# Sample tokens' expert dots, the second group's query blocks and state products, and the closings of three tiles moved to other slots of a hand-written order

## What is computed

```python
q = (xb @ w_q).reshape(blk, PEER_HEADS, 2, half)            # "wq" jobs, 8 heads of 256 columns
...                                                         # q normalised per half
s = jnp.einsum('thpd,hpnd->thpn', q, keys_f)                # "scores"
s1, i1 = lax.top_k(s[:, :, 0], PEER_TOPK); s2, i2 = ...     # 16 of 128, twice
sc, ci = lax.top_k(cand, PEER_TOPK)                         # 16 of 256: the head's experts
h = jax.nn.gelu(jnp.einsum('thkd,td->thk', u_tab[idx], xb)) # "dots"
y = jnp.einsum('thk,thkd->td', gate * h, v_tab[idx])        # "sums"
x2 = LN(alpha*x1 + y);  x3 = x2 + (p @ w_pe) * sigmoid(x2 @ w_pg)   # "closing" of a tile
```

## Time and profile before

| | |
|---|---|
| median of 3 runs | 1877.51 us (1875.82 to 1878.71) |
| the profiled execution's own time | 1876.79 us |
| its span | 1875.0 us |
| busy: PE, DVE, POOL, ACT | 76%, 63%, 54%, 22% |
| DMA | 673.28 MB, mean 359 GB/s |
| mean granted TensorE clock | 0.842 of full speed |

### The profile page before, as it was taken

One profiled execution on the slowest core, in us unless ns is written; L12 is line 12 of the kernel. 1 busy time (PEld: TensorE's weight loads), 2 busy tenths in 40 slices (PEclk: granted clock), 3 DMA queues, 4 the chain that ended last, 5 costly groups with the idle time before them and its releaser, 6 DMA issues.

```text
span 1875.0 us, 20726 instructions
## 1 busy us (share of the span) xinstructions
PE 1424.7 (76%) x7144; PEld 890.3 (47%) x7144; DVE 1172.9 (63%) x3013; ACT 418.0 (22%) x848; POOL 1003.4 (54%) x1067
## 2 busy tenths in 40 slices
PE   8999999799878798989894997356643435775477
PEld 7888887676654455656461554023311001241034
DVE  1110224878877674776678665788888967776632
ACT  2320201124431122232111222111321211031022
POOL 0000000646655565665466766576777776767764
PEclk9999999899997799999896998658765666587589
DMA  7335551999999999999999999999999999999996
GB/s 293 135 122 217 223 179 52 329 413 404 411 412 412 407 413 409 407 411 411 394 395 410 379 410 413 408 408 407 407 410 409 408 407 395 395 362 410 409 396 269
DMA packets 173494, 673.28 MB, mean 359 GB/s; under 512 B 20768, under 2 KB 24480, under 8 KB 159567
## 3 DMA queue, kind: packets, MB, share of 16 engines
q0 software_dynamic: 151520, 546.94, 73.9%
q1 hardware_dynamic: 21798, 124.96, 17.1%
q10 hardware_dynamic: 72, 0.07, 0.0%
HBM read 664.48 MB, written 7.41 MB: 358 GB/s over the span
## 4 chain that ended last, share of the span: by engine, by line
PE 42%; DMA 26%; DVE 14%; POOL 10%; issue 7%; ACT 1%; SPq 0%; DVEq 0%; POOLq 0%; PEldq 0%
DMA at<-in_v_tab,idxV 18%; PE PJ L1633 14%; PE PJ L1513 7%; PE Y L1683 7%; DMA at<-in_u_tab,idx 7%; POOL at L746 5%; DVE at L1382 5%; POOL at L755 5%; PE PJ L1497 4%; PE PJ L1520 3%; PE PJ L1532 1%; DVE at L1310 1%; PE Y L1722 1%; PE PJ L1539 1%; PE PJ L1586 0%
## 5 line engine op out<-in xcount | busy, mean ns | idle before, releaser
L746 POOL DMA_INDIRECT at<-in_u_tab,idx x512 | 489.8, 957 | 556.6 <-DVEq L1365 322.7
L1382 DVE CUSTOM_DVE_ANT_0 at<-at,XD 128x1024 f32<-128x1024 f32 x512 | 615.9, 1215 | 202.7 <-DMA at<-in_u_tab,idx 189.4
L755 POOL DMA_INDIRECT at<-in_v_tab,idxV x512 | 487.6, 952 | 290.3 <-PE Y L1683 156.0
L1683 PE MATMUL Y<-at,at 128*32 128x512 f32 x1920 | 340.5, 837 | 371.3 <-DMA at<-in_v_tab,idxV 371.1
L1633 PE MATMUL PJ<-at,at 128*128 128x256 f32 (+1 forms) x1792 | 413.9, 390 | 6.3 <-DVE at L1232 2.3
L1633 PEld LDWEIGHTS PJ<-at,at 128*128 128x128 f32 x1792 | 342.0, 193 | 86.3 <-issue 23.7
L1683 PEld LDWEIGHTS Y<-at,at 128*32 128x32 f32 x1920 | 69.9, 135 | 554.8 <-issue 553.7
L1513 PE MATMUL PJ<-at,at 128*128 128x256 f32 (+2 forms) x960 | 218.5, 386 | 2.5 <-DVE at L1289 1.0
L1513 PEld LDWEIGHTS PJ<-at,at 128*128 128x128 f32 (+2 forms) x960 | 166.5, 176 | 57.7 <-issue 14.8
L1497 PE MATMUL PJ<-at,at 128*128 128x256 f32 (+1 forms) x640 | 142.0, 380 | 0.0
L1497 PEld LDWEIGHTS PJ<-at,at 128*128 128x128 f32 (+1 forms) x640 | 107.6, 170 | 36.0 <-issue 9.2
(11 more groups left out here) (237 smaller groups left out, 1350.7 us busy)
## 6 DMA issues: line engine op xcount, KB each, us to landing
at<-in_w_blk SPq DMA_DIRECT2D x72, 1024.0 KB, 7.9
at<-in_w_q SPq DMA_DIRECT2D x16, 1024.0 KB, 8.0
at<-in_w_o SPq DMA_DIRECT2D x8, 1024.0 KB, 7.3
at<-in_u_tab,idx POOLq DMA_INDIRECT x512, 11.6
at<-in_v_tab,idxV POOLq DMA_INDIRECT x512, 11.0
at<-in_state SPq DMA_DIRECT2D x4, 1024.0 KB, 8.6
out_st_s<-at SPq DMA_DIRECT2D x4, 1024.0 KB, 8.8
at<-in_w_pg SPq DMA_DIRECT2D x2, 2048.0 KB, 14.0
```

The lines of the kernel that those rows point to most:

```text
L746: pool.indirect_dma_start(ubuf[slot], None, u_tab, bass.IndirectOffsetOnAxis(rows_of, 0)).then_inc(u_in[slot], 16)
L755: pool.indirect_dma_start(vbuf[slot], None, v_tab, bass.IndirectOffsetOnAxis(rows_of, 0)).then_inc(v_in[slot], 16)
L1382: v.tensor_tensor_reduce(out=t, in0=t, in1=XD[:, :], scale=1.0, scalar=0.0, op0=ALU.mult, op1=ALU.add, accum_out=hraw[:, n % 2, k:k + 1]). ...
L1683: last = mm(Y[32 * c:32 * c + 32, s, :], wpadV[d // PAIR % 2][:, g, :], vbuf[slot][:, 512 * s:512 * s + 512], start=False, stop=final)
```

## The change

- `SAMPLE_DOTS_AT` 26, every second slot, becomes 25, every fourth slot (`SAMPLE_STEP`): samples 0 to 7 at slots (25, 0), (25, 4), ... (26, 12), two steps ("two heads") instead of one. `sample_at` says which sample stands at a slot; the gathers of GpSimd, their numbering (`u_number`, `u_sample`) and the row jobs follow it.
- `REST_AT`: the closing of tile 0 starts at slot (20, 1) instead of (18, 1), tile 1 at (22, 1) instead of (20, 1), tile 2 at (27, 6) instead of (27, 1). Tile 4 stays at (30, 1).
- `queries(1)` runs by pairs of heads, tile by tile, instead of head by head, and the 23 jobs are spread to slot (18, 7) instead of (15, 15).
- The planner's cost of a state product ("outer") is 3.5 instead of 1.4, so each gets more slots; what stands before them comes up to 4 slots earlier, what stands behind up to 7 slots later, fading to 1 slot at step 13.
- SP loads the second norm's rows at the first query job of tile 2 instead of at the last query job of all; `w_pg`, `w_pe` and p stay behind the last query job, which is now at slot (18, 4) instead of (15, 14).

```diff
-SAMPLE_DOTS_AT, SAMPLE_SUMS_AT = 26, 28
-REST_AT = {0: 18, 1: 20, 2: 27, NT: 30}
+SAMPLE_DOTS_AT, SAMPLE_SUMS_AT, SAMPLE_STEP = 25, 28, 4
+REST_AT = {0: (20, 1), 1: (22, 1), 2: (27, 6), NT: (30, 1)}
+
+
+def sample_at(n, k):
+
+    b, odd = divmod(TOPK * (n - SAMPLE_DOTS_AT) + k, SAMPLE_STEP)
+    return b if odd == 0 and b in range(S) else None
@@ def queries(g):
-    return [("job", g, "wq", i, j) for i in range(PH) for j in TILES[g]]
+    return [("job", g, "wq", 2 * b + i, j) for b in range(PH // 2) for j in TILES[g] for i in range(2)]
@@ def cost(e):
-                "outer": 1.4, "os": 3.2, "sk": 1.0, "t1": 1.0, "t2": 1.0, "normv": 0.9, "norm1": 0.9}.get(e[2], 3.6)
+                "outer": 3.5, "os": 3.2, "sk": 1.0, "t1": 1.0, "t2": 1.0, "normv": 0.9, "norm1": 0.9}.get(e[2], 3.6)
@@ def plan():
-    behind.update(spread_over(wq2[1:], (13, 10), (15, 15)))
+    behind.update(spread_over(wq2[1:], (13, 10), (18, 7)))
...
     for j, at in REST_AT.items():
-        behind.setdefault((at, 1), []).append(("order", j))
+        behind.setdefault(at, []).append(("order", j))
         for k, e in enumerate(rest(j)):
-            behind.setdefault((at, k + 2), []).append(e)
+            behind.setdefault(divmod(TOPK * at[0] + at[1] + 1 + k, TOPK), []).append(e)
             if e[2] == "pe":
-                behind.setdefault((at, k + 4), []).append(("take", e))
+                behind.setdefault(divmod(TOPK * at[0] + at[1] + 3 + k, TOPK), []).append(("take", e))
...
-            if n == SAMPLE_DOTS_AT and k % 2 == 0:
-                out.append(("sample dot", k // 2))
+            if sample_at(n, k) is not None:
+                out.append(("sample dot", sample_at(n, k)))
...
-            b = (TOPK * (n - SAMPLE_DOTS_AT) + k + 1) // 2
-            if k % 2 and b in range(S):
-                out += [("job", 1, "row", b, s) for s in range(2)]
+            if sample_at(n, k + 1) is not None:
+                out += [("job", 1, "row", sample_at(n, k + 1), s) for s in range(2)]
@@ def u_number(n, k):
-    before = k // 2 + 1 if n == SAMPLE_DOTS_AT + 1 else S if n > SAMPLE_DOTS_AT else 0
-    return n * TOPK + k + before
+    behind = (n - SAMPLE_DOTS_AT - 1) * TOPK + k
+    return n * TOPK + k + (min(behind // SAMPLE_STEP + 1, S) if behind >= 0 else 0)
@@ def u_sample(b):
-    return U_SAMPLE + 3 * b
+    return U_SAMPLE + (SAMPLE_STEP + 1) * b
@@ program.sync
-                    if e == ("job", 1, "wq", PH - 1, NT):
+                    if e == ("job", 1, "wq", 0, NT - 2):
                         sp.wait_ge(x1_ok, NT + 1)
                         load_rows(ln2_g, ln2_b, ln2_in)
+                    if e == ("job", 1, "wq", PH - 1, NT):
                         sp.wait_ge(pj_done, JOB[e] + 1)
@@ program.gpsimd
-                    if n == SAMPLE_DOTS_AT and k % 2 == 0:
-                        gather_u(u_sample(k // 2), idxT[:, FIRST + k // 2:FIRST + k // 2 + 1])
+                    b = sample_at(n, k)
+                    if b is not None:
+                        gather_u(u_sample(b), idxT[:, FIRST + b:FIRST + b + 1])
```

## The result

The changed kernel takes 1888.88 us (median of 4 runs, 1887.81 to 1889.79), the kernel before in the same series 1877.43 us: ratio 1.0061, 95% interval 1.0049 to 1.0073. That is 11.5 us slower, outside the range given. Its profiled execution took 1889.79 us, with a span of 1888.0 us against 1875.0 before.

A forecast was written before the change was run, and what follows sets the result against it. It took the DMA stream (409 GB/s) as the bound, cushioned only by issued, unlanded gathers. Tile 2's closing -2.0, +0.5 for what may remain, step 30 -1.0: -2.5 us, median 1875.0 us, range 1869.5 to 1881.0.

The forecast's parts named there:

- state products, and all that moves by up to 7 slots in steps -1 to 13: Steps -1 to 13: the stream is full, so moving this work costs 0, with 2 us either way.
- of the kind of 3.93 us that left no mark: POOL's wait at 1271.92 us left GB/s at 408 and 407; waits moved with state products were taken as equally harmless.
- The samples: Steps 25 and 26: one POOL wait of about 2 us in each, inside the cushion; gain 0, bound -2.6.
- Rival 2: Slots (25, 0) to (26, 12): row pairs behind sums hold DVE and so POOL; 1885 us, chance 0.09.
- Closing of tile 2: Around 1660 to 1680 us: sums late by less than the cushion; gain 2.0 us, less 0.5 for what may remain.
- step 30: Last closing: starting from a thicker gather queue, it gains 1.0 us (at least 0).
- landing reading: Dips valued by gathers' issue-to-landing times, since consumers wait for landings; tile 2's closing lost 2.0 us, step 30 1.0.
- byte reading: Dips valued by mean bytes missed against 409 GB/s: 4.9 us at 1660 to 1680, 2.6 at 1590 to 1600.
- rival 1: The byte reading holds at samples, tile 2's closing and step 30: -6.1 us, 1871.4 us; chance 0.24.
- Query jobs: Steps 13 to 18: total work stays and the stream is full, so thinning gains 0; bounds -3.6 and +3.
- rival 3: Thinned query jobs run at half clock: 1879.5 us, or 1891 with the second job slow too; chance 0.10.
- cushion of 6.0 us: Steps 22 to 25: work queued in issued, unlanded gathers; a POOL wait shorter than that costs nothing.

The follow-up runs named there:

- e2: Kernel before with only the planner's cost of a state product at 3.5 instead of 1.4: 1891.57 us, ratio 1.0076.
- e1: Changed kernel with the planner's cost of a state product back at 1.4, all else kept: 1876.52 us, 0.9994 of the kernel before.
- e14: Kernel before with only the 68 events ahead of the first state product moved 1 to 5 slots earlier: 1887.16 us, ratio 1.0056.
- e6: Changed kernel with everything ahead of the first state product at its old slots, the rest by cost 3.5: 1879.95 us, ratio 1.0013.
- e8: Kernel before with cost 3.5 and half of PE's products omitted in first group's queries and second group's q, k, v, r: 1881.46 us, ratio 1.0023.
- e10: Kernel before with only the planner's cost of a state product at 2.1 instead of 1.4: 1882.67 us, ratio 1.0018.
- e9: Kernel before with only the planner's cost of a state product at 0.7 instead of 1.4: 1883.81 us, ratio 1.0027.
- e15: Kernel before with the front kept, only state products and what stands behind them laid out by cost 3.5: 1878.90 us, ratio 1.0013.
- e3: Kernel before with only the closing of tile 2 started at slot (27, 6) instead of (27, 1): 1876.35 us, ratio 0.9998.
- e11: Changed kernel with cost back at 1.4 and the samples' closing at slot (29, 8) instead of (30, 1): 1876.31 us, ratio 0.9991.
- e5: Kernel before with only the query blocks, closings of tiles 0 and 1 and norm rows' load moved as in the change: 1878.32 us, 1.0002.

## Why the prediction was wrong, point by point

**The step that failed** is the term for "state products, and all that moves by up to 7 slots in steps -1 to 13", set at "0, with 2 us either way". It measured +14.8 us alone (e2) and +12.4 in the changed kernel (1888.88 less e1's 1876.52). Two things were wrong in it. The first: I took from a full stream that there was room for work to come earlier. The stream only says that sums and dots were not yet late. What PE still waits ahead of its sums was there to read. PE's waits on v gathers in the kernel before, in 345 to 530, 600 to 1060 and 1060 to 1560 us (us in total, times, longest):

```profile
PE Y L1683 <- DMA at<-in_v_tab,idxV: 6.3, 3, 3.1
...
PE Y L1683 <- DMA at<-in_v_tab,idxV: 59.6, 16, 10.0
...
PE Y L1683 <- DMA at<-in_v_tab,idxV: 201.6, 35, 16.7
```

In the first stretch PE is late or just in time at seven of its ten sums, with 6.3 us to spare in 185; that is where the front was pulled in. (PE's one long wait there, 7.4 us for DVE at 352 us, stands ahead of the first of these sums and was still 7.5 us in the changed kernel.) A step takes about 45 us there (the first dots of two steps that are five apart start at 372.8 and 599.3), a slot thus 2.8, and PE has hardly a pause: five slots earlier is 5 x 2.8 = 14 us of PE's work ahead of sums and dots that had stood before it. Less some cushion, that is 10 us. This estimate was made after the fact and is only of the right size; e14 (+11.2), e6 (the front put back, +2.1 left) and e8 (1.0 instead of 10.7 by 588 us) carry the finding. It holds for the front: between 588 and 881 us e10 and e9 lost 6.7 and 9.1 us more, although PE has 27.7 us of waits on v gathers in 600 to 880 us of the kernel before. Why is open, as are the 3.0 us of e15.

The second: I called the moved waits "of the kind of 3.93 us that left no mark". The length of a wait of POOL doesn't tell its cost. The longest of 1050:1300 in the kernel before is 8.03 us, as long as the one at 425.91, and the rate is whole:

```profile
1175.00:1185.00 10.00, 3.10 (x16) 0.69 (x16) 4.92 (x8) 0.00 (x0) 0.94 (x1) 0.51 1.03 407
...
1181.90 3.32 PE L1683 MATMUL Y<-at,at 128*32 128x512 f32 x16 [16.71 <-DMA at<-in_v_tab,idxV]
...
1185.47 0.93 POOL L755 DMA_INDIRECT at<-in_v_tab,idxV  x1 [8.03 <-PE Y L1683]
```

There PE itself had waited 16.71 us for the landing, behind 5 MB of weight loads that SP had issued at 1153.65, 12 us of the stream at 409 GB/s: the DMA engines had other work, and POOL's wait cost nothing. At 425.91 PE came to the sum out of more than 17 us of products without a wait: PE was late, and the rate fell to 318. But that PE waited for a landing doesn't make a wait of POOL harmless by itself: at 1820.09 in the changed kernel (below) it had, and the rate was 274. What differs between these three places is whether the DMA engines had enough other work.

**The samples:** 0 was right (0.9996). POOL's longest wait on a dot between 1560 and 1645 us is 2.0 us where it had been 3.23, as foretold, though DVE waits for the row jobs in ten places (17.4 us) and not in up to eight. The dip of 303 at 1590 is gone (410), but 1610:1620 and 1620:1640 have 376 and 385 instead, and at equal bytes nothing is won or lost over them (13.6 at 544 MB, 14.0 at 592). Rival 2 didn't happen.

**Closing of tile 2 and step 30:** in the closing the mechanism held and the landing reading fell. In the changed kernel, 1660:1680, and POOL's waits in 1645 to 1700 us:

```profile
1660.00:1680.00 20.00, 14.49 (x79) 9.12 (x80) 12.62 (x27) 4.32 (x10) 15.00 (x16) 0.84 1.03 407
...
POOL at L761 <- PE Y L1690: 4.3, 2, 3.8
```

The longest wait is 3.8 us for 6.65, the u gathers of 1690 to 1740 us land after a median of 8.2 us for 6.9, all as foretold. But what it is worth is read by bytes: 4.3 us in e3 between 592 and 616 MB, close to the 4.9 of the byte reading and not to my 2.0. And yet the time hardly moved. The medians of e3, e1 and e11 allow a gain of at most 2.1, 2.8 and 3.2 us (the lower ends of their intervals) and show none clear of noise, so rival 1's 6.1 us are ruled out, while the -2.5 of the sum is not quite. Part of the answer is step 30: I gave it -1.0 for a thicker queue, and it went the other way. Between 648 and 656 MB (1796 to 1817 us) the changed kernel loses 1.8 us on the kernel before, e1 1.4, e11 2.7 and e3 0.5. A wait removed 200 us before the end is then met again, in part, where the last sums are late; this is read from single profiles, and no run holds step 30 fixed. The changed kernel pays here:

```profile
1820.00:1830.00 10.00, 6.49 (x52) 1.98 (x56) 0.39 (x2) 3.90 (x10) 4.68 (x5) 0.83 0.78 274
...
1820.09 3.61 PE L1690 MATMUL Y<-at,at 128*32 128x512 f32 x16 [4.69 <-DMA at<-in_v_tab,idxV]
...
1823.93 0.94 POOL L761 DMA_INDIRECT at<-in_v_tab,idxV  x1 [4.34 <-PE Y L1690]
```

The profile of e3 also lost 2.1 us between 544 and 592 MB, ahead of anything that its edit touches; single profiles differ by as much there (e15, with nothing of the closings moved, lost 1.7 between 544 and 568 MB).

**Query jobs:** 0 was right (1.0002). The mean granted clock in 1060:1560 is 0.73 in e5 and in the kernel before; in 1030:1160, where the jobs had been dense, it fell from 0.94 to 0.85. The Trainium skill, "TensorE: Matmul & The Clock Gate", Part 1, has the throttled clock as the default that activity lifts; by it more jobs should have run at half clock. The trace agrees, and gives the size: the 384 products of these jobs kept PE busy for 95.7 us in e5 where they had taken 89.5. In 1060 to 1560 PE waits 201.6 us on landings, so there was cover for these 6.2 us, and of rival 3's price (+2.0 to +13.5) nothing shows in the time.

**The range** took in 2 us either way for a term that moved more than a hundred events. The rivals were all drawn from the places with a dip; none asked what happens where work is added to a stretch without one. That the samples and the query jobs came out at 0 was foretold with its reasons and is not luck; that the closing of tile 2 is worth 4.3 us by bytes and next to nothing in time was not foretold.

## What to carry to other kernels

Before moving work earlier in a fixed order, add up per stretch how long the engine that is to take it still waits ahead of its deadlines (here PE's waits on landings ahead of the sums, and the dots that hang on PE's products by way of ACT and DVE). Where that was near zero, most of the time pulled in came out again at the end, however full the transfers looked. The reverse isn't shown: a stretch with waits to spare is no proof of room (e9 and e10). A wait of the engine that issues the transfers cost nothing where the DMA engines had other work to last through it, and cost time where they had not, whatever ended it; read the rate beside it. A planner's cost of one kind of job moves everything ahead of it as well; try it with the front held in place.

## What the runs showed of the hardware

A gather's landing time overstates how much work stands in the queue. In 1400 to 1580 us the last of its 16 shares arrives 11.5 us after the issue, the median share after 5.5 to 6 us (counted from the completion events of the kernel before's trace). In 325 to 345 us, with the queue nearly empty, these are 5.8 and 4.6 us. So the cushion of 6.0 us that I read as 11.7 less 5.7 was for half of the engines only about 1 us. The Trainium skill, "DMA: Bandwidth & Descriptors", in the section on why a DMA increments its semaphore by 16, says that the 16 engines finish independently; the trace agrees, and gives the distance. It fits with what the bytes showed at tile 2's closing.
